# Three of the eight expert blocks at 64 token slots, their high and low halves side by side in one stationary tile

## The chip, the cores and the metric

The kernel runs on one core of one Trainium2 chip. The metric is the device time of one execution in microseconds (us), taken as the median of several runs. The core has TensorE (PE in the profile, its weight loads are PEld), VectorE (DVE), ScalarE (ACT), GpSimd (POOL) and SyncE (SP), which issues nearly all DMAs here.

## The reference, cut to what matters

A decoder of three layers on 256 tokens of width 1024: forgetting attention and a dense SwiGLU; a conformer convolution and a mixture of experts; differential and stick-breaking attention and a squared-ReLU network. All is float32. The change touches the mixture alone.

```python
def moe_swiglu(h, w_router, w_gate, w_up, w_down):     # T = 256, D = 1024, 8 experts, top 2, EXPERT_FF = 3584
    logits = (xt @ w_router).astype(jnp.float32)
    top_logit, top_idx = lax.top_k(logits, TOP_K)
    gates = jax.nn.softmax(top_logit, axis=-1)
    ...
    def expert_block(args):                             # one block of up to 128 tokens of one expert
        xb, e = args
        return (silu(xb @ w_gate[e]) * (xb @ w_up[e])) @ w_down[e]
    ...
    ys = ys * gate_buf[:, None]                         # gate-weighted, added back to the tokens
```

With the reference's own inputs (worked out from its router on the host, no measurement) the eight experts get 87, 54, 67, 80, 49, 43, 66 and 66 of the 512 assignments. None has more than 128, so there are eight blocks. The three smallest of experts 1 to 7 are 5, 4 and 1, with 43, 49 and 54.

## The kernel before

**Exact products.** TensorE multiplies float32 in its fast form only if the operands are rounded. So every operand is split in two: ScalarE writes the rounded, high part (`wh`, `xh`, `ah`), VectorE writes what is left (`wl`, `xl`, `al`; helper `rest`, L2052), and `exact` (L1354 to L1356) adds three products: high by high, high by low, low by high.

**Units.** Weights come as units of 1 MiB (128 partitions by 2048 floats). SP loads each into one of six slots of `raw`; a slot is loaded again when VectorE has split the unit in it (`lo_ready` of six units earlier). ScalarE splits unit j+3 into one of three slots of `wh` when TensorE has finished unit j (`unit_done`), VectorE follows when ScalarE has (`hi_ready`), TensorE when VectorE has (`lo_ready`).

**Blocks.** An expert block is 42 units in the order of `MOE_ORDER`: for each of seven chunks of 512 hidden columns (c = 0 to 6) two halves of gate (g), two of up (u) and, one chunk late, two of down (d). So a chunk is g g u u d d, the down units being those of the chunk before. The tokens' rows, transposed, are the stationary operand (`xgh`, `xgl`, 128 token slots), weights move in 512 columns, and each unit takes 4 pieces x 3 products = 12 matmuls. After g1 ScalarE takes silu of the gate product out of PSUM (L1192); after u1 VectorE multiplies it by the up product (L2539); TensorE turns the 128 by 512 result with four transposes (`turned`, L1839, issued after g1 of the next chunk); ScalarE and VectorE split it (`turned_hi` L1186, `turned_lo`), and the down units use it.

**Loops.** A block number `i` runs over `nb` blocks, read from a register once routing is planned. TensorE and VectorE have one loop over blocks; ScalarE's is turned by a third of a block (`ACT_TURN`), so that it can drain a finished block (L1207) a little into the next. Weight loading is one loop on SP, which takes block i's expert number from `etab`, stores the block's result rows (`y_rows`) at unit 12 of the next and loads the next block's token rows (`x_blk`) at unit 20. `x_rows` and `y_rows` lie in DRAM; their unused rows are zeroed early (`zero_rows`).

**Around the blocks.** Block 0 is expert 0. Its rows are gathered on TensorE by `gather`, a product of the normalised tokens `z_tok` with a selection matrix `sel`. VectorE first plans: `oh` marks each token's experts, `mcum` (TensorE) counts, `kcol` is each assignment's row, `sel` marks the rows of block 0, `kidx` is the list for GpSimd's scatter into `x_rows`, then come `etab`, `nbt` (the numbers of blocks), the gate values, `kept` and `yidx`. Then VectorE splits the gathered rows and the unit `co3`+3, which is unit 2 of block 0, and enters its loop. After the seventh block GpSimd gathers all blocks but the last from `y_rows` (four indirect DMAs), scales by the gates and adds (L784 to L789) while the last block runs; TensorE adds that to the last block's part (`tokens_of_earlier_blocks`, `scatter`).

The set of instructions on each engine is written out by hand in program order; nothing reorders it, and every engine but TensorE's weight loads works it off in that order.

## Time and profile before

| | us |
|---|---|
| median of 3 runs | 1835.2 (1834.9 to 1836.87) |
| span of the profiled execution, first to last instruction | 1835.6 |
| TensorE busy in it | 1801.9 (98%) |
| VectorE busy | 1405.0 (77%) |
| ScalarE busy | 1163.9 (63%) |
| expert loads | 336 of 1 MiB, eight blocks of 42 |

The page gives no other time for the profiled execution, so its span stands for it; it lies 0.4 us over the median. Windows of a trace give busy time, the granted TensorE clock (PEclk, 1.00 is 2.4 GHz and 0.50 is 1.2 GHz) and what the DMA engines moved. "Idle before" is the time that an engine stood before such an instruction, with what ended it.

### The profile page before, as it was taken

Reading aid. Unit: us, or ns where it says so; the run is one execution under the profiler, and the core shown is the slowest. Engines: PE = TensorE matmul, PEld = TensorE weight load, DVE = VectorE, ACT = ScalarE, POOL = GpSimd, SP = SyncE. Lnnn points to the kernel's source line nnn. Section 1 sums busy time; section 2 is a strip of 40 time slices with the busy share of each in tenths; the row PEclk is TensorE's granted clock in tenths of the full one; section 3 lists DMA queues with packets and bytes.
Section 4 is the critical chain, followed back from the end, with each engine's and each line's share of the span. In section 5 each row is a group of like instructions: output and inputs, shape, how many; then the busy total and the mean of one; then the engine's idle time right before and its main releaser. Section 6 shows DMA issues by size and latency. Waiting matters only on the chain.

```text
span 1835.6 us, 28123 instructions
## 1 busy us (share of the span) xinstructions
PE 1801.9 (98%) x10836; PEld 1598.3 (87%) x10836; DVE 1405.0 (77%) x1329; ACT 1163.9 (63%) x1149; POOL 229.4 (12%) x194
## 2 busy tenths in 40 slices
PE   8999999999999999999999999999999999899998
PEld 8988999998878888888888888888887899799997
DVE  6665877679678888888889888888889857665553
ACT  6765434457667777777777777777776757543332
POOL 0462111302020000000000000000007011302221
PEclk9999999999989999999999999999999999999998
DMA  9633888831359999999999999999999943235530
GB/s 391 270 122 145 310 333 328 315 138 39 123 223 385 367 393 381 366 399 373 383 385 374 393 374 370 389 375 392 374 367 420 371 161 138 93 115 184 184 138 24
DMA packets 75407, 523.27 MB, mean 285 GB/s; under 512 B 8296, under 2 KB 8448, under 8 KB 14784
## 3 DMA queue, kind: packets, MB, share of 16 engines
q1 hardware_dynamic: 73056, 514.02, 73.4%
q0 software_dynamic: 2272, 8.15, 1.2%
q8 instruction: 56, 0.92, 0.2%
q14 instruction: 23, 0.19, 0.0%
HBM read 506.38 MB, written 15.75 MB: 284 GB/s over the span
## 4 chain that ended last, share of the span: by engine, by line
PE 93%; DVE 4%; ACT 2%; issue 1%; DMA 0%; POOL 0%; DVEq 0%; SPq 0%; ACTq 0%
PE ps L1354 27%; PE ps L1356 27%; PE ps L1355 27%; DVE wl L2052 1%; PE ps L1677 1%; PE ps L1839 1%; PE ps L1384 1%; ACT wh L828 1%; PE ps L1532 1%; DVE big L2045 1%; PE ps L1368 1%; PE ps L1549 1%; PE ps L1488 0%; PE ps L1377 0%; DMA big<-in_mem 0%
## 5 line engine op out<-in xcount | busy, mean ns | idle before, releaser
L2052 DVE TENSOR_TENSOR wl<-raw,wh 128x2048 fp32r<-128x2048 f32 x446 | 1026.2, 2303 | 261.8 <-ACT wh L828 148.5
L1180 ACT ACTIVATE wh<-raw 128x2048 fp32r<-128x2048 f32 x336 | 644.5, 1919 | 181.8 <-PE ps L1356 181.2
L1354 PE MATMUL ps<-wh,xh 128*128 128x512 f32 (+1 forms) x1040 | 396.3, 381 | 1.7 <-DVE wl L2052 1.7
L1356 PE MATMUL ps<-wh,xl 128*128 128x512 f32 (+1 forms) x1040 | 390.0, 375 | 0.0
L1355 PE MATMUL ps<-wl,xh 128*128 128x512 f32 (+1 forms) x1040 | 389.5, 375 | 0.0
L1354 PE MATMUL ps<-xh,wh 128*128 128x256 f32 x1120 | 321.9, 287 | 5.4 <-DVE xl L2052 3.5
L828 ACT ACTIVATE wh<-raw 128x2048 fp32r<-128x2048 f32 x107 | 204.4, 1910 | 178.2 <-PE ps L1356 174.3
L1355 PE MATMUL ps<-xl,wh 128*128 128x256 f32 x1120 | 317.2, 283 | 0.0
L1356 PE MATMUL ps<-xh,wl 128*128 128x256 f32 x1120 | 317.2, 283 | 0.0
L1354 PEld LDWEIGHTS ps<-wh,xh 128*128 128x128 f32 x1040 | 195.8, 188 | 37.9 <-DVE wl L2052 2.9
L1356 PEld LDWEIGHTS ps<-wh,xl 128*128 128x128 f32 x1040 | 195.7, 188 | 35.6
L1355 PEld LDWEIGHTS ps<-wl,xh 128*128 128x128 f32 x1040 | 195.9, 188 | 33.9 <-issue 0.5
L1354 PEld LDWEIGHTS ps<-xh,wh 128*128 128x128 f32 x1120 | 215.4, 192 | 9.3 <-issue 6.0
L1355 PEld LDWEIGHTS ps<-xl,wh 128*128 128x128 f32 x1120 | 215.3, 192 | 0.6 <-issue 0.5
L1356 PEld LDWEIGHTS ps<-xh,wl 128*128 128x128 f32 x1120 | 215.1, 192 | 0.0
L1354 PE MATMUL ps<-wh,ah 128*128 128x512 f32 x448 | 175.8, 392 | 1.1 <-DVE al L2052 1.1
L1356 PE MATMUL ps<-wh,al 128*128 128x512 f32 x448 | 174.6, 390 | 0.0
L1355 PE MATMUL ps<-wl,ah 128*128 128x512 f32 x448 | 174.4, 389 | 0.0
L1354 PE MATMUL ps<-ah,wh 128*128 128x256 f32 x496 | 142.2, 287 | 0.4 <-POOL al L738 0.2
L1355 PE MATMUL ps<-al,wh 128*128 128x256 f32 x496 | 140.7, 284 | 0.0
L1356 PE MATMUL ps<-ah,wl 128*128 128x256 f32 x496 | 140.6, 283 | 0.0
L738 POOL TENSOR_TENSOR al<-att_p,ah 128x512 fp32r<-128x512 f32 x27 | 74.8, 2771 | 337.9 <-ACT ah L1040 337.9
(327 smaller groups left out, 1978.0 us busy)
## 6 DMA issues: line engine op xcount, KB each, us to landing
raw<-in_experts SPq DMA_DIRECT2D x336, 1024.0 KB, 7.0
raw<-in_units SPq DMA_DIRECT2D x134, 1024.0 KB, 5.3
x_rows<-big SPq DMA_DIRECT2D x1, 6144.0 KB, 36.0
big<-x_rows SPq DMA_DIRECT2D x8, 512.0 KB, 7.8
y_rows<-big SPq DMA_DIRECT2D x7, 512.0 KB, 8.5
y_rows<-big SPq DMA_DIRECT2D x1, 2560.0 KB, 41.7
sqz<-gate_rows POOLq DMA_DIRECT2D x12, 192.0 KB, 4.3
big<-in_mem SPq DMA_DIRECT2D x1, 1024.0 KB, 7.1
```

The lines of the kernel that those rows point to most:

```text
L738: pool.tensor_tensor(al[:, c % 2, :], sg[:, c % 2, :], ah[:, c % 2, :].bitcast(F32), ALU.subtract).then_inc(sem("hid_lo"), 1)
L828: act.activation(wh[:, p % SPL, :], raw[:, n % RAW, :], ACT.Copy).then_inc(sem("hi_ready"), 1)
L1180: act.activation(wh[:, p % SPL, :], raw[:, n % RAW, :], ACT.Copy).then_inc(sem("hi_ready"), 1)
L1354: mm(out_, lh, rh, start=start, stop=False, **kw)
L1355: mm(out_, lh, rl, start=False, stop=False, **kw)
L1356: return mm(out_, ll, rh, start=False, stop=stop, **kw)
L1368: ins = pe.transpose(bank(name)[:, at:at + P], src, ident)
L1384: ins = mm(bank(f"nsum{k}")[:, t:t + 1], src[:, at:at + P], ones[:, 0:1], start=(c == 0 and t == 0), stop=(c == KT - 1), skip_group_check= ...
L1532: ins = mm(s[:, at:at + nk], m["q"][:, P * t:P * t + P], m["k"][:, 0:nk], start=True, stop=True)
L1549: mm(o, m["v"][0], pT[:, 0:T], start=True, stop=False, skip_group_check=True)
L1677: mm(bank(f"conv{c}")[:, 0:T], diag[:, n % DIAG_RING, :], upad[:, c, tap:tap + T], start=(tap == 0), stop=(n + 1 == taps_through(PE_CONV, ...
L2052: return V.tensor_tensor(out_, whole, leading.bitcast(F32), ALU.subtract)
```

## The change

Blocks are numbered anew. Expert 0 stays block 0. The other seven are ranked by their counts on the chip (`order`, `rank`); the three smallest become blocks 1, 3 and 5 with 64 token slots each ("thin"), the next three blocks 2, 4 and 6, the largest block 7. The loops of TensorE, VectorE and ScalarE run three times over a pair (a full block, a thin block), and then over the remaining full blocks.

In a thin block the stationary tile is `thin_x`: columns 0 to 63 are the high halves of 64 tokens, columns 64 to 127 their low halves. Each unit takes two products for each piece, with `wh` and with `wl`, so 8 matmuls and no third product. The partitions of the result are then 64 rows by the high and 64 by the low half, which must be added. For gate and up ScalarE copies both products out of PSUM (`thin_gate`, `thin_up`), and TensorE multiplies each by a constant `fold` (128 by 64, two unit matrices above each other): eight float32 matmuls with 64 moving columns, which add the halves and turn the tile at once. Silu, product and split then work on 256 columns. For the down product the halves are not added on the chip's block: both are stored in `y_rows`, and GpSimd gathers twice, first the low halves of thin blocks into `y_low` (after block 5 is stored; other tokens read a zero row), then as before and adds.

```diff
@@ zero_rows (SP)
-                sp.dma_start(y_rows[E - 1:MAXBLK + 1, :, :]...
+                sp.dma_start(y_rows[2 * THIN:MAXBLK + 1, :, :]...
@@ gpsimd
+            pool.wait_ge(sem("y_stored"), 2 * THIN * 16 + 1)
...
-                                            bass.IndirectOffsetOnAxis(yidx[:, a, t:t + 1], 0)).then_inc(
+                                            bass.IndirectOffsetOnAxis(ylow[:, a, t:t + 1], 0)).then_inc(
...
+                pool.tensor_tensor(y_low[:, t, :], y_got[0][:, t, :], y_got[1][:, t, :],
+                                   ALU.add).then_inc(sem("y_low"), 1)
+            pool.wait_ge(sem("y_low"), TT)
+            pool.wait_ge(sem("y_stored"), last * 16 + 1)
...
+                pool.tensor_tensor(y_low[:, t, :], y_low[:, t, :], y_got[0][:, t, :], ALU.add).then_inc(sem("y_low"), 1)
+                pool.wait_ge(sem("y_low"), TT + t + 1)
+                pool.tensor_tensor(y_kept[:, t, :], y_low[:, t, :], y_got[1][:, t, :],
@@ scalar, thin_units
+                for j in range(first, end):
+                    kind, c, half = MOE_ORDER[j]
+                    if (kind, half) == ("g", 1) and c >= 1:
+                        folded_hi(c - 1)
...
+                    if kind in "gu" and half == 1:
+                        act.wait_ge(sem("unit_done"), past(MOE_UNITS) + POS0 + j + 1)
+                        taken_to, b = (thin_gate, 2 * (c % 2)) if kind == "g" else (thin_up, 2 * (c % 2) + 1)
+                        act.activation(taken_to[:, c % 2, :], ps[:, b, :], ACT.Copy).then_inc(sem("thin_taken"), 1)
+                    split_unit(j, past)
+                    if (kind, half) == ("g", 0) and c >= 1:
+                        folded_silu(c - 1)
@@ tensor, thin_block
+                def both(out_, rows, w, start, stop):
+
+                    mm(out_, rows, w[0], start=start, stop=False)
+                    return mm(out_, rows, w[1], start=False, stop=stop)
+
+                def folded(c):
+
+                    pe.wait_ge(sem("thin_taken"), own(2 * MOE_CH) + 2 * c + 2)
+                    psum, done = spare(f"T{c}", past)
+                    for g, src in enumerate((thin_gate, thin_up)):
+                        for f in range(4):
+                            at = THIN_CAP * (4 * g + f)
+                            ins = mm(psum[:, at:at + THIN_CAP], src[:, c % 2, P * f:P * f + P], fold, start=True, stop=True)
...
+                        if half == 0:
+                            pe.wait_ge(sem("thin_lo"), own(MOE_CH) + c + 1)
...
+                    if (kind, half) == ("g", 0) and c >= 1:
+                        folded(c - 1)
@@ vector, the plan
+            for t in range(TT):
+                V.tensor_scalar(sel[:, t, :], iota, plan_f[:, 1, E * t:E * t + 1], plan_f[:, 0, E * t:E * t + 1],
+                                ALU.is_equal, ALU.mult).then_inc(sem("moe_sel"), 1)
...
+            link(stt(order, cnt, float(E), cc(C_RANK, E), ALU.mult, ALU.add))
+            link(V.tensor_tensor(lt8[:, :, :], inner(order), outer(order), ALU.is_lt))
+            link(V.tensor_reduce(rank, lt8[:, :, :], AX_X, ALU.add))
...
+            gathered_rest(1)
             dve.wait_ge(sem("moe_keys"), 1)
...
+            split_after("co3")
+
+            link(V.tensor_tensor(through, before, over, ALU.add))
@@ vector, thin_block
+                for j, (kind, c, half) in enumerate(MOE_ORDER):
...
+                    split_unit(j, past)
+                    if (kind, half) == ("g", 0) and c >= 1:
+                        folded_product(c - 1)
+                    if (kind, half) == ("g", 1) and c >= 1:
+                        folded_lo(c - 1)
```

**ScalarE, one chunk of a block.** Before, L1180 is the split of a weight unit, L1192 the silu after g1 and L1186 the turned hidden tile's high half.

```order
L1191 REGISTER_ALU
L1192 ACTIVATE att_p<-ps 128x512 [waits unit_done]
L1180 ACTIVATE wh<-raw 128x2048 [waits unit_done,ring_loaded4]
L1185 ISA
L1186 ACTIVATE ah<-ps 128x512 [waits moe_filled7]
L1179 REGISTER_ALU [waits ring_loaded5]
L1180 ACTIVATE wh<-raw 128x2048 [waits unit_done]
```

Now, in a thin block, L1213 is the split of a weight unit, L1253 the silu and L1259 the high half of the folded hidden tile, L1272 a copy of a product out of PSUM; `moe_drained6` is given by VectorE's product.

```order
L1253 ACTIVATE att_p<-ps 128x256 [waits moe_filled6]
L1258 REGISTER_ALU
L1259 ACTIVATE ah<-att_p 128x4x64 [waits moe_drained6]
L1270 REGISTER_ALU
L1272 ACTIVATE att_p<-ps 128x512 [waits unit_done]
L1213 ACTIVATE wh<-raw 128x2048 [waits unit_done,ring_loaded4]
L1212 REGISTER_ALU [waits ring_loaded5]
L1213 ACTIVATE wh<-raw 128x2048 [waits unit_done]
```

The high half and a copy now stand ahead of the split of g1's third-next unit, and the high half waits for VectorE.

**VectorE, the same place.** L2201 is the rest of a weight unit, L2756 the product of silu and up, the row behind L2761 the rest of the folded tile.

```order
L2201 TENSOR_TENSOR wl<-raw,wh 128x2048 [waits hi_ready]
L2756 TENSOR_TENSOR att_p<-att_p,ps 128x256 [waits thin_silu]
L2714 REGISTER_ALU
L2201 TENSOR_TENSOR wl<-raw,wh 128x2048 [waits hi_ready]
L2761 REGISTER_ALU
L2201 TENSOR_TENSOR ah<-att_p,ah 128x4x64 [waits moe_hid_hi]
```

The product stands behind a weight unit's rest, and the next row is a rest that waits for ScalarE.

**VectorE, the plan.** Behind the rest of the second gathered half comes the unit of `co3`+3, and then what is left of the plan, down to `ylow`, before the loop's first weight unit (first rows and last):

```order
L2201 TENSOR_TENSOR xl<-ps,xh 128x512 [waits gather_hi]
L2663 CAST kidx<-kcol 128x4 [waits moe_keys]
L2201 TENSOR_TENSOR wl<-raw,wh 128x2048 [waits hi_ready]
L2666 TENSOR_TENSOR plan_f<-plan_f 128x8
L2667 TENSOR_SCALAR pexp<-plan_f 128x1 [waits dve_step]
...
L2706 TENSOR_SCALAR klow<-klow 128x4 [waits dve_step]
L2707 CAST ylow<-klow 128x4 [waits dve_step]
L2779 UNCONDITIONAL_BRANCH
```

Some thirty small instructions now stand between that unit and the loop, where four stood before; of those ahead of it some twelve are new or moved.

## Rows read from the trace of the kernel before

**Rows 1.** The page: busy time (share of the span) of each engine.

```profile
PE 1801.9 (98%) x10836; PEld 1598.3 (87%) x10836; DVE 1405.0 (77%) x1329; ACT 1163.9 (63%) x1149; POOL 229.4 (12%) x194
```

**Rows 2.** Groups by line, 640 to 1360 us: xcount | busy us, mean ns | idle before.

```profile
L2052 DVE TENSOR_TENSOR wl<-raw,wh 128x2048 fp32r<-128x2048 f32 x256 | 585.8, 2289 | 85.6 <-ACT wh L1180 85.6
L1180 ACT ACTIVATE wh<-raw 128x2048 fp32r<-128x2048 f32 x256 | 491.2, 1919 | 135.4 <-PE ps L1356 135.4
L1354 PE MATMUL ps<-wh,xh 128*128 128x512 f32 x685 | 269.9, 394 | 0.0
L1192 ACT ACTIVATE att_p<-ps 128x512 f32<-128x512 f32 x43 | 25.8, 599 | 34.5 <-PE ps L1356 34.5
```

**Rows 3.** Timeline in a full block: start us, us, engine, line.

```profile
640.57 0.39 PE L1354 MATMUL ps<-wh,xh 128*128 128x512 f32 x1
640.77 1.92 ACT L1180 ACTIVATE wh<-raw 128x2048 fp32r<-128x2048 f32 x1 [0.80 <-PE ps L1356]
641.25 0.39 PE L1354 MATMUL ps<-wh,xh 128*128 128x512 f32 x1
...
642.72 2.29 DVE L2052 TENSOR_TENSOR wl<-raw,wh 128x2048 fp32r<-128x2048 f32 x1 [0.43 <-ACT wh L1180]
...
646.21 0.60 ACT L1192 ACTIVATE att_p<-ps 128x512 f32<-128x512 f32 x1 [0.80 <-PE ps L1356]
...
646.70 1.91 ACT L1180 ACTIVATE wh<-raw 128x2048 fp32r<-128x2048 f32 x1
...
648.64 4.53 DVE L2052 TENSOR_TENSOR wl<-raw,wh 128x2048 fp32r<-128x2048 f32 x2 [0.91 <-ACT wh L1180]
```

**Rows 4.** Timeline of ScalarE: the drains of two blocks that follow each other.

```profile
650.75 1.06 ACT L1207 ACTIVATE big<-ps 128x512 f32<-128x512 f32 x2
769.22 1.06 ACT L1207 ACTIVATE big<-ps 128x512 f32<-128x512 f32 x2
```

**Rows 5.** Small operations elsewhere: timeline, and the last from the chain.

```profile
480.80 0.40 ACT L1135 ACTIVATE xh<-big 128x256 fp32r<-128x256 f32 x1
481.36 0.42 DVE L2052 TENSOR_TENSOR xl<-big,xh 128x256 fp32r<-128x256 f32 x1
503.28 0.98 PE ps L1384 x8
```

**Rows 6.** Stretches: us, busy us of each engine, granted clock, DMA share, GB/s.

```profile
14.00:17.00 3.00, 0.66 (x6) 0.45 (x5) 2.96 (x6) 1.21 (x3) 0.00 (x0) 1.00 0.99 414
17.00:21.00 4.00, 4.00 (x35) 4.00 (x36) 4.00 (x12) 2.62 (x7) 0.00 (x0) 1.00 1.02 421
512.00:515.00 3.00, 0.01 (x1) 0.00 (x0) 2.67 (x16) 2.98 (x5) 0.00 (x0) 0.93 0.00 0
515.00:518.00 3.00, 2.75 (x13) 2.78 (x14) 2.06 (x17) 0.35 (x2) 1.70 (x2) 0.50 0.13 52
```

**Rows 7.** The plan: VectorE's timeline, ScalarE's `z_tok`, and the chain's gather.

```profile
511.43 2.42 ACT L1161 ACTIVATE big<-ps,rcol 128x512 f32<-128x512 f32 x4 [0.62 <-DVE rcol L2083]
515.19 0.17 DVE L2493 TENSOR_TENSOR plan_f<-plan_f 128x8 f32<-128x8 f32 x1
515.25 6.73 PE ps L1786 x32
527.12 2.29 DVE L2052 TENSOR_TENSOR wl<-raw,wh 128x2048 fp32r<-128x2048 f32 x1 [0.89 <-ACT wh L1180]
```

**Rows 8.** A stretch in which the loads lag behind.

```profile
1400.00:1410.00 10.00, 8.92 (x42) 7.04 (x41) 9.08 (x5) 7.40 (x6) 9.92 (x3) 1.00 1.02 424
```

**Rows 9.** Timeline of the last block's end pieces and of GpSimd's pass in it.

```profile
1342.27 0.60 PE L1847 MATMUL ps<-cst,big 128*128 128x128 f32 x4
1403.05 2.58 POOL L789 TENSOR_TENSOR big<-big 128x1024 f32<-128x1024 f32 x1
1411.43 11.43 DVE L2052 TENSOR_TENSOR wl<-raw,wh 128x2048 fp32r<-128x2048 f32 x4
1464.03 0.60 PE L1847 MATMUL ps<-cst,big 128*128 128x128 f32 x4
```

More of the change, by code:

```diff
@@ L71 @@
 MAXBLK = E + EXTRA
+THIN = 3
+THIN_CAP = CAP // 2
+SLOT_OF_RANK = ([2 * r + 1 for r in range(THIN)] + [2 * f + 2 for f in range(THIN)]
+                + list(range(2 * THIN + 1, E)) + [0])
 FF2 = 4096
@@ L96 @@
 C_XI = C_LT + E * E
-C_END = C_XI + EXTRA * E
+C_FOLD = C_XI + EXTRA * E
+C_RANK = C_FOLD + THIN_CAP
+C_SLOT = C_RANK + E
+C_END = C_SLOT + E
 def constants():
@@ L322, in build @@
         y_kept = y_got[0]
+        y_low = view(0, TT, D, sqz)
         sq4 = big[:, 5888:7936]
@@ L1840, in turned @@
                     ins.then_inc(done, 1)
-                def next_rows(g):
-                    psum, done = spare(f"G{g}")
-                    for f in range(4):
-                        at = 512 * g + P * f
-                        ins = pe.transpose(psum[:, P * f:P * f + P], x_blk[:, at:at + P], ident)
-                    ins.then_inc(done, 1)
                 for j, (kind, c, half) in enumerate(MOE_ORDER):
                     if j < 2:
-                        b = MOE_BANK[f"G{half}"][0]
-                        pe.wait_ge(sem(f"moe_drained{b}"), i * len(MOE_USES[b]) + 1)
+                        rows_ready(half, past)
                     if kind in "gu":
                         b = 2 * (c % 2) + (kind == "u")
-                        w = unit(j, 4)
+                        w = moe_unit(j, 4, past)
                         for k in range(4):
@@ new lines, in _ @@
+            with pe.Fori(0, THIN) as i:
+                fat_block(lambda per: i * (2 * per), lambda per: i * per)
+                thin_block(lambda per: i * (2 * per) + per, lambda per: i * per)
+            pe.wait_ge(sem("moe_plan"), 2)
+            nb = pe.value_load(nbt[0:1, 0:1], min_val=E, max_val=MAXBLK)
+            more = pe.value_load(nbt[0:1, 2:3], min_val=E - 2 * THIN, max_val=MAXBLK - 2 * THIN)
+            with pe.Fori(0, more) as i:
+                fat_block(lambda per: i * per + 2 * THIN * per, lambda per: i * per + THIN * per)
@@ L2461, in _ @@
             dve.wait_ge(sem("moe_marks"), 1)
-            pos = plan_f[:, 1, :]
-            cnt = bank("mcum")[:, 2 * E:3 * E]
+            pos, cnt, order, rank = plan_f[:, 1, :], plan_f[:, 4, 0:E], plan_f[:, 2, 0:E], plan_f[:, 3, 0:E]
+            thin, cap, place, over = plan_f[:, 6, 0:E], plan_f[:, 7, 0:E], plan_f[:, 8, 0:E], plan_f[:, 11, 0:E]
+            before, past_cap, through = plan_f[:, 5, 0:E], plan_f[:, 16, 0:E], plan_f[:, 15, 0:E]
             V.tensor_tensor(pos, bank("mcum")[:, 0:2 * E], marks, ALU.subtract)
-            link(stt(lt8[:, :, 0:E], cnt.unsqueeze(1).broadcast_to([P, E, E]), float(CAP),
-                     cc(C_LT, E * E).rearrange("p (a b) -> p a b", a=E), ALU.is_gt, ALU.mult))
@@ L2473, in _ @@
-            link(V.tensor_tensor(two(12), two(10), plan_f[:, 11, 0:E].unsqueeze(1).broadcast_to([P, TT, E]), ALU.add))
+            V.tensor_copy(cnt, bank("mcum")[:, 2 * E:3 * E]).then_inc(drained("mcum"), 1)
+            wait_drained(dve, "mcum")
+            iota = cc(C_IOTA, CAP)
+            for t in range(TT):
+                V.tensor_scalar(sel[:, t, :], iota, plan_f[:, 1, E * t:E * t + 1], plan_f[:, 0, E * t:E * t + 1],
+                                ALU.is_equal, ALU.mult).then_inc(sem("moe_sel"), 1)
@@ new lines, in _, with gathered_rest @@
+            link(V.tensor_tensor(lt8[:, :, :], inner(over), cc(C_LT, E * E).rearrange("p (a b) -> p a b", a=E), ALU.mult))
+            def gathered_rest(j):
+                dve.wait_ge(sem("gather_hi"), j + 1)
+                rest(four_of(xgl, j), bank(f"gather{j}"),
+                     four_of(xgh, j)).then_inc(sem(f"moe_drained{MOE_BANK[f'G{j}'][0]}"), 1)
+            gathered_rest(0)
+            link(V.tensor_reduce(before, lt8[:, :, :], AX_X, ALU.add))
+            link(V.tensor_tensor(past_cap, before, place, ALU.subtract))
```

327 lines of the change are left out of this document (230 added, 97 removed).

## The prediction

> **What bounds the kernel now.** I read the page first: TensorE is busy for 1801.9 of 1835.6 us, VectorE for 1405.0, ScalarE for 1163.9 [rows 1]. Busy alone is no bound, so I looked at who waits in the stretch from 640 to 1360 us, where six blocks run alike. The reader is to see three things there [rows 2]. TensorE's matmuls have no idle time before them. VectorE stood 85.6 us, always for ScalarE, and ScalarE stood 135.4 us, always for TensorE. So TensorE sets the pace and the other two follow it. Its matmuls of 512 columns start 0.227 us apart (three in 0.68 us, [rows 3]), a unit of 12 takes 2.73 us, and a block takes 118.47 us, drain to drain [rows 4], or 16.9 us for a chunk of six units.
>
> Then I asked how far behind the followers are. ScalarE's split takes 1.92 us, VectorE's rest 2.29 us [rows 3]. Where two rests follow each other without a wait they take 4.53 us together, 2.24 each (I use 2.21 for one in a longer run: the second starts 0.08 before the first has ended). Six of them are 13.3 us of the chunk's 16.9. The loads are close too: with loads lagging, the DMA engines move 424 GB/s [rows 8], so 1 MiB needs 2.48 us, and a block with its rows 42 x 2.48 + 2 x 1.28 = 106.7 us.
>
> **The change, part by part.** *TensorE in a thin block.* A unit falls from 12 to 8 matmuls, 8 x 0.227 = 1.82 us. A fold is eight float32 products, each two records. The nearest row for records that small is 0.98 us for 8 [rows 5], so 16 x 0.1225 = 1.96 us; its streaming alone could be half of that. A chunk is 6 x 1.82 + 1.96 = 12.9 us instead of 16.9. If TensorE alone counted, three blocks would save 3 x 7 x 4 = 84 us. It doesn't: the followers now lead.
>
> *The circle in a thin chunk.* I follow VectorE through one chunk, in program order. It does the rest of g0's third-next unit, and behind it the product of 256 columns (0.42 us by [rows 5], 0.35 when next in line). Only then may ScalarE make the high half, since it waits for that product; behind the high half stands the copy of the gate product, and only behind that the split that VectorE needs next. So VectorE stands for 0.31 (high half, 0.40 in [rows 5] less overlap) + 0.49 (copy: 646.21 to 646.70 in [rows 3]) + 1.92 (split) and three hand-overs of some 0.05 (642.69 to 642.72 in [rows 3] is one): 2.9 us. The rest is work: 6 x 2.21 + 2 x 0.35 = 13.96. Together **16.85 us per thin chunk, against 16.9 of a full one**. ScalarE and TensorE fit into the circle: after the standstill VectorE's rests lie back to back, and from a rest (TensorE starts), through a unit (8 matmuls, the last ending 0.39 after its start: 2.0), the split (1.92) to the third-next rest there are 0.3 to 0.4 us to spare in each turn. So by its works alone a thin block lasts 118.3 +- 1.5 us, three of them save 0 (from -5 to +5, if the copy, product or halves are a quarter shorter or longer). The loads need 106.7 and stay hidden.
>
> *The clock.* TensorE has 16.9 - 12.9 = 4.0 us idle in each thin chunk, and most of it in one piece: it has done u1 when VectorE comes out of its standstill, and d0 needs VectorE's rest of that unit and the folded rest behind it. That is 3.1 us; 0.3 before each following unit are the remainder. What do such gaps do? After a stretch with 0.66 of 3.0 us busy (a gap of 2.3 us) the clock stayed at 1.00; after one with 0.01 of 3.0 us busy it was at 0.50 [rows 6], that is 1.2 for 2.4 GHz. Mine lies between them, nearer to the second in length, and it comes 21 times. If the clock falls, the unit behind the gap takes 8 x 0.427 = 3.4 us instead of 1.8 (512 columns at 1.2 GHz are 0.427), 1.6 later; 0.35 is spare, so the circle grows by 1.25 us: 21 x 1.25 = +26 us. I take this, since the gap repeats in the same place and once the clock is down the rest of that chunk is later still; bounds 0 and, with a fall that covers two units each time, 21 x 2.6 = 55 us.
>
> The Trainium skill (TensorE: Matmul & The Clock Gate, Why this matters for your kernels) speaks against the change here: thin matmul bursts parted by waits make the clock oscillate, once with each burst. By that rule the sum is the 1868 below, without it 1841; the trace of before has no such repeated bursts and cannot show it.
>
> *The plan.* `sel` is made some 2 us earlier, but the gather also needs `z_tok`, whose last copy ends at 513.85; it began at 515.25 [rows 7]. So it starts at most 1.2 us earlier. VectorE doesn't follow: after the second gathered half (about 522) come `kidx`, the rest of unit 2 (to 524.5) and some 30 instructions of 0.17 us [rows 7], 5.1 us, so the rest of unit 3 begins at 529.6 instead of 527.12 and ends at 531.9. TensorE had begun unit 3 at 521.98 + 3 x 2.73 = 530.2. **+2 us**, from 0 (small instructions overlap) to 3.5. `kidx` and GpSimd's scatter are 7 us later; the rows are read 17 units later, hidden. Queued behind the plan on VectorE is only its loop.
>
> *GpSimd's second pass.* The last block lasted 1464.03 - 1342.27 = 121.76 us between equal pieces [rows 9], 3.3 more than 118.47, with GpSimd's gather and sums beside it: four rests took 11.43 us there instead of 8.8. Block 6 now gets such a pass too, +3.3, and block 7's has two more additions of 2.58 us; at the same 30% they cost VectorE 1.5, +1.2 after its slack. **+4.5 us**, from 1 (if only the last block feels it) to 8. SP's zeroing is 0.5 MB longer at about 60 us, where loads have idle DMA before them; 0. The waits for `moe_plan` go from ahead of the block loops to behind the first three pairs; VectorE had long given the signal when TensorE ended its gather at 521.98: 0.
>
> The sum against the runs' median (the span is 0.4 more): 1835.2 + 0 + 26 + 2 + 4.5 = **1867.7**, I say 1868.
>
> **The rivals.** *The clock holds.* For it: 3.1 us is shorter than the gap that is known to bring it down, and full work surrounds it. Then 1835.2 + 2 + 4.5 - 0.5 = 1841, 1836 to 1846. Chance 0.20.
>
> *Thin blocks run at VectorE's or the loads' pace (faster).* If the standstill isn't there (ScalarE runs ahead, hand-overs overlap), VectorE needs 42 x 2.21 + 14 x 0.35 + 1.4 = 99 us, loads 106.7, and the block would be 106.7: 3 x 11.8 = 35 saved, 1835.2 - 35 + 6.5 = 1806; half of it gives 1824. For it: VectorE has 13.9 us of work in a chunk. Against: ScalarE's program order. It decides from a standstill under 2.3 us, where a thin chunk beats a full one by enough for the 6.5 us. Chance 0.13.
>
> *The clock stays down longer* (slower still): 1835.2 + 55 + 6.5 = 1897. Chance 0.05. *It doesn't do what it says*: with more than 64 tokens for a thin expert there is a ninth block, +118, 1953. The counts 43, 49 and 54 speak against it. Chance 0.01. The forecast keeps 0.61, from 1853 (half of the gaps bring the clock down) to 1880 (all do, and both other bounds).
>
> **How the numbers follow.** The range takes in the forecast's bounds and the first rival's lower end, 1834 to 1880: 0.61 + 0.19 and little of the second. A measurement of this kernel can tell about 0.2%, 3.7 us, from no change. Faster by more: the second rival, 0.13. Within 1831.5 to 1838.9: the low part of the first, 0.06. Slower: 0.81.
>
> **What would show it.** In the trace after: the distance of two drains with a thin block between them, 118 + 127 us for a pair if I am right, 118 + 118 if the clock holds, 118 + 107 if the second rival is. VectorE's wait before a weight rest, for ScalarE, of 2.9 us once in a thin chunk; ScalarE's wait for VectorE's product before the high half; TensorE's wait for the folded rest of 3.1 us or more seven times a block; granted clock under 1.00 in thin blocks alone. The start of unit 3 near 532, and some 121 us for blocks 6 and 7. The prediction is wrong if VectorE has no such wait, or if the clock stays at 1.00.

## The result, and the profile after

The changed kernel took 1888.05 us (median of four runs, 1887.33 to 1888.5), the kernel before in the same comparison 1835.05 (1833.1 to 1836.87): 1.0288 times the time, 95% interval 1.0275 to 1.0301. It is slower, as forecast, but by 53 us and not by 33, and the time lies above the range. The profiled execution took 1887.85 us, with a span of 1886.0. In all runs whose span is on record it is 1.8 to 1.9 us shorter than the time, so the execution of before whose profile was kept, with its span of 1835.6, took about 1837.4 us and was 2.4 slower than its median. That is why the spans below differ by 50.4 us and the medians by 53.

The page's busy line of after, where [rows 1] stood for before, says that TensorE is busy for 33 us less and that this was no use:

```profile
PE 1769.3 (94%) x10584; PEld 1562.6 (83%) x10584; DVE 1402.5 (74%) x1350; ACT 1167.6 (62%) x1188; POOL 274.2 (15%) x207
```

The groups by line of after from 640 to 1360 us (count | busy us, mean ns | idle before and who ended it) answer to [rows 2]. Before, TensorE's matmuls had no idle time there. Now one group of the thin blocks, the first products of unit d0 with the folded tile, has 64.9 us, and VectorE stands longer for ScalarE:

```profile
L2201 DVE TENSOR_TENSOR wl<-raw,wh 128x2048 fp32r<-128x2048 f32 x243 | 555.7, 2308 | 120.0 <-ACT wh L1213 119.6
L1213 ACT ACTIVATE wh<-raw 128x2048 fp32r<-128x2048 f32 x243 | 460.6, 1914 | 125.4 <-PE ps L1447 67.6 <-PE ps L1984 54.2 <-DMA raw<-in_experts 3.3
L1983 PE MATMUL ps<-wh,ah 128*128 128x512 f32 x168 | 88.6, 527 | 64.9 <-DVE ah L2201 64.9
```

The timeline of after in one thin chunk (start us, us, engine, line, what ended the idle time) shows the circle that the prediction drew:

```profile
686.25 0.41 DVE L2756 TENSOR_TENSOR att_p<-att_p,ps 128x256 f32<-128x256 f32 x1
686.69 0.42 ACT L1259 ACTIVATE ah<-att_p 128x256 fp32r<-128x256 f32 x1 [2.79 <-DVE att_p L2756]
687.02 0.58 ACT L1272 ACTIVATE att_p<-ps 128x512 f32<-128x512 f32 x1
687.49 3.70 ACT L1213 ACTIVATE wh<-raw 128x2048 fp32r<-128x2048 f32 x2
...
689.43 2.29 DVE L2201 TENSOR_TENSOR wl<-raw,wh 128x2048 fp32r<-128x2048 f32 x1 [2.77 <-ACT wh L1213]
...
691.64 0.42 DVE L2201 TENSOR_TENSOR ah<-att_p,ah 128x256 fp32r<-128x256 f32 x1
...
692.21 0.57 PE L1983 MATMUL ps<-wh,ah 128*128 128x512 f32 x1 [3.25 <-DVE ah L2201]
```

VectorE gives the product at 686.66, ScalarE waited 2.79 us for it, and then it makes the high half, the copy and only then the split; VectorE stands 2.77 us; TensorE gets the folded rest after 3.25 us of waiting. The stretches of after around it (us, busy of PE, PEld, DVE, ACT, POOL, granted clock, DMA share, GB/s) show what that gap costs: full clock up to it, half (1.2 GHz) for most of the next 4 us, then full again.

```profile
686.00:689.00 3.00, 2.96 (x14) 2.10 (x12) 0.66 (x2) 2.31 (x3) 0.00 (x0) 1.00 0.99 358
689.00:692.00 3.00, 0.00 (x0) 0.00 (x0) 2.57 (x3) 3.00 (x4) 0.00 (x0) 1.00 0.87 325
692.00:696.00 4.00, 3.79 (x10) 3.00 (x11) 4.00 (x3) 1.68 (x2) 0.00 (x0) 0.57 0.80 296
696.00:703.00 7.00, 7.00 (x41) 6.05 (x40) 5.71 (x4) 5.72 (x4) 0.00 (x0) 1.00 1.02 424
```

The drains of after, beside [rows 4] (a thin block between the first two, a full one between the next):

```profile
659.53 1.06 ACT L1285 ACTIVATE big<-ps 128x512 f32<-128x512 f32 x2
793.20 1.06 ACT L1285 ACTIVATE big<-ps 128x512 f32<-128x512 f32 x2
910.06 1.06 ACT L1285 ACTIVATE big<-ps 128x512 f32<-128x512 f32 x2
```

A pair takes 250.5 us instead of 236.9. How the 250.5 divide between the thin and the full block depends on where a block is said to begin. I mark blocks by the end of VectorE's rest of their first unit, read from the timeline of each kernel:

| us | before | after | products added (e3_fill) | split first (e2_split_first) |
|---|---|---|---|---|
| start of block 0 | 492.55 | 501.02 | 501.23 | 500.21 |
| block 0 | 146.66 | 148.55 | 148.47 | 148.56 |
| blocks 1 to 5 | 592.33 | 628.41 | 596.18 | 566.84 |
| of them the thin ones | (118.47) | 130.39, 127.54, 129.42 | 117.89 each | 107.73, 107.77, 107.80 |
| block 6 | 118.46 | 120.80 | 122.82 | 123.77 |
| block 7 | 121.76 | 125.12 | 124.71 | 125.00 |

So the 50.4 us by which the span grew are 8.5 before the experts, 1.9 in block 0, 36.1 in blocks 1 to 5, 2.3 and 3.4 in the last two blocks, and 1.7 less behind them. The marks leave one thing out. In before the clock was at half from 504 to 508 us, behind the mark of block 0, and in after from 477 to 481, ahead of it; neither kernel has the other's fall:

```profile
504.00:508.00 4.00, 4.00 (x14) 1.48 (x14) 0.00 (x0) 0.28 (x1) 0.00 (x0) 0.57 0.00 0
```

```profile
477.40:480.80 3.40, 3.40 (x8) 2.77 (x9) 1.42 (x4) 0.00 (x0) 0.00 (x0) 0.50 0.51 214
```

The lateness of after against before, matmul by matmul, is therefore 0.7 us from 30 us on, 6.2 behind the stretch of 70 to 90 us, 6.8 from 200 us on, 8.5 at the mark, 6.85 again just ahead of the gather of block 0, and 10.4 in block 0 behind its third unit.

### The profile page after: what moved, and what is told of

It is laid out like the page before. It is cut to its first block, busy times and chain, and to the rows that moved or that the text cites. A ratio compares the mean times of both kernels' runs of the same rounds, so it can differ in the third digit from the quotient of the medians.

```text
span 1886.0 us, 27737 instructions
## 1 busy us (share of the span) xinstructions
PE 1769.3 (94%) x10584; PEld 1562.6 (83%) x10584; DVE 1402.5 (74%) x1350; ACT 1167.6 (62%) x1188; POOL 274.2 (15%) x207
## 4 chain that ended last, share of the span: by engine, by line
PE 75%; DVE 9%; issue 7%; ACT 6%; DMA 2%; POOL 1%; DVEq 0%; ACTq 0%; SPq 0%
PE ps L1445 20%; PE ps L1447 19%; PE ps L1446 19%; DVE wl L2201 5%; ACT wh L1213 4%; PE ps L1983 4%; PE ps L1984 3%; PE ps L1768 1%; PE ps L1475 1%; PE ps L1993 1%; PE ps L1943 1%; DMA raw<-in_experts 1%; ACT wh L867 1%; PE ps L1468 1%; DMA sqz<-gate_rows 1%
## 5 line engine op out<-in xcount | busy, mean ns | idle before, releaser
L2201 DVE TENSOR_TENSOR wl<-raw,wh 128x2048 fp32r<-128x2048 f32 x446 | 1029.9, 2323 | 300.0 <-ACT wh L1213 148.5
L1213 ACT ACTIVATE wh<-raw 128x2048 fp32r<-128x2048 f32 x336 | 638.9, 1915 | 186.0 <-PE ps L1447 128.2
L1445 PE MATMUL ps<-wh,xh 128*128 128x512 f32 (+1 forms) x704 | 265.9, 378 | 15.2 <-DVE wl L2201 10.6
L1447 PE MATMUL ps<-wh,xl 128*128 128x512 f32 (+1 forms) x704 | 259.9, 369 | 0.0
L1446 PE MATMUL ps<-wl,xh 128*128 128x512 f32 (+1 forms) x704 | 259.6, 369 | 0.0
L1445 PEld LDWEIGHTS ps<-wh,xh 128*128 128x128 f32 x704 | 133.2, 189 | 41.6 <-DVE wl L2201 13.7
L1447 PEld LDWEIGHTS ps<-wh,xl 128*128 128x128 f32 x704 | 133.0, 189 | 22.6
L1446 PEld LDWEIGHTS ps<-wl,xh 128*128 128x128 f32 x704 | 133.4, 189 | 21.3 <-issue 0.5
L1983 PE MATMUL ps<-wh,ah 128*128 128x512 f32 x168 | 88.6, 527 | 64.9 <-DVE ah L2201 64.9
L1983 PE MATMUL ps<-wh,xh 128*128 128x512 f32 x336 | 134.6, 401 | 2.3 <-DVE wl L2201 1.8
L1984 PE MATMUL ps<-wl,xh 128*128 128x512 f32 x336 | 131.4, 391 | 0.0
## 6 DMA issues: line engine op xcount, KB each, us to landing
y_rows<-big SPq DMA_DIRECT2D x1, 3072.0 KB, 43.2
```

The source lines that it names most:

```text
L1213: act.activation(wh[:, p % SPL, :], raw[:, n % RAW, :], ACT.Copy).then_inc(sem("hi_ready"), 1)
L1445: mm(out_, lh, rh, start=start, stop=False, **kw)
L1446: mm(out_, lh, rl, start=False, stop=False, **kw)
L1447: return mm(out_, ll, rh, start=False, stop=stop, **kw)
L1983: mm(out_, rows, w[0], start=start, stop=False)
L1984: return mm(out_, rows, w[1], start=False, stop=stop)
```

## Experiments on the thin blocks

**Fill the gap.** If it is the clock that makes a thin chunk 18.4 us (the six long waits of TensorE in the first thin block end 18.4 us apart on average), useless work in the gap must make it shorter.

```diff
+FILL = 3
...
@@ tensor, thin_block
                     else:
+                        if half == 0:
+                            for _ in range(FILL):
+                                mm(ps[:, 2 * (c % 2), :], ident, cc(0, 512), start=True, stop=True)
                         w = moe_unit(j, 2, past)
                         if half == 0:
```

> The changed kernel, with three float32 products of 512 columns on constants added on TensorE in each thin chunk, ahead of its wait for unit d0, into an unused bank; the output is the same. They fill the gap with work that nobody needs. Theory (21 falls of the clock are what makes a thin block 129 us instead of 118, VectorE's circle does the rest): the clock stays at 1.00 in thin blocks, a thin block lasts 118.5, three of them 33 us less, the full blocks behind them 4 less, the time 1852 to 1857. Rival (the clock's fall costs nothing on the path, the handovers do): 1888, or more by the products' own time, 21 x 2.6 = 54.

Measured: 1858.04 us (1855.39 to 1861.0), 1.0122 times before, interval 1.0101 to 1.0143, 1 us over the expected range. The timeline of this kernel has the added products where the gap was (first row: the last three of the six records that the three products leave):

```profile
670.81 1.45 PE L2009 MATMUL ps<-cst 128*128 128x512 f32 x3
...
673.60 0.47 PE L1984 MATMUL ps<-wh,ah 128*128 128x512 f32 x1 [1.34 <-DVE ah L2205]
```

A stretch of thin blocks, of after and then of this kernel:

```profile
670.00:775.00 105.00, 84.59 (x354) 69.47 (x355) 79.69 (x46) 71.24 (x58) 0.00 (x0) 0.84 0.92 355
```

```profile
660.00:750.00 90.00, 85.98 (x381) 63.03 (x382) 75.34 (x44) 69.17 (x56) 0.00 (x0) 1.00 0.98 388
```

The clock is 1.00 instead of 0.84, and each thin block takes 117.89 us, 16.84 a chunk. Adding work that nobody needs made the kernel 30 us faster. VectorE's standstill is still there (2.77 us); what is left is the circle's own length, which the prediction had worked out as 16.85. That the two agree to 0.01 us is in part luck: inside the block the products of d0 lie 16.74 us apart, and the block's ends make the rest. The full blocks behind the thin ones, expected 4 us shorter in all, did not get shorter.

**Take the circle apart.** One call moves on ScalarE:

```diff
@@ scalar, thin_units
                 for j in range(first, end):
                     kind, c, half = MOE_ORDER[j]
+                    split_unit(j, past)
                     if (kind, half) == ("g", 1) and c >= 1:
                         folded_hi(c - 1)
...
-                    split_unit(j, past)
```

> The changed kernel, with one edit in the thin blocks: after g1 ScalarE makes the split of the third-next weight unit first, and only then the high half of the folded tile and the copy of the gate product. Nothing is left out. Theory (VectorE's standstill of 2.8 us in each thin chunk is ScalarE's program order, and it makes the gap of 3.2 to 3.9 us on TensorE behind which the clock falls): the standstill shrinks to under 1 us, the clock stays at 1.00 in thin blocks, a thin block lasts 107 to 111 us instead of 129, and the time is 1826, from 1815 to 1851 (the upper end if the loads lag). Rival (thin units themselves, small matmuls and waits, are what is slow): 1885 to 1888.

Measured: 1829.44 us (1826.24 to 1836.6, eight runs), 0.9967 times before, interval 0.9951 to 0.9983. The timeline of this kernel in a thin chunk: VectorE stands 0.76 us instead of 2.77, and TensorE 1.13 instead of 3.25.

```profile
682.87 2.29 DVE L2201 TENSOR_TENSOR wl<-raw,wh 128x2048 fp32r<-128x2048 f32 x1 [0.76 <-ACT wh L1213]
...
685.65 0.47 PE L1983 MATMUL ps<-wh,ah 128*128 128x512 f32 x1 [1.13 <-DVE ah L2201]
```

Its stretch of a thin block:

```profile
660.00:750.00 90.00, 81.30 (x396) 63.79 (x395) 83.70 (x49) 77.66 (x63) 0.00 (x0) 1.00 1.01 416
```

A thin block takes 107.8 us, clock 1.00, and the DMA engines have no idle share left. That is close to the 106.7 that the second rival of the prediction had for the loads, but the loads do not set the whole pace. A chunk takes 14.87 us from early in the block on, which is VectorE's 13.96 us of work and the some 0.8 for which it still stands; ScalarE's splits waited for a load only 8 times between 640 and 1220 us, 3.8 us in all:

```profile
ACT wh L1213 <- DMA raw<-in_experts: 3.8, 8, 0.6
```

VectorE and the loads are about level here. The waits of TensorE in the experts (us in total, times, longest), of after, with the products and with the split first, put the three side by side. Of the 21 places of after 18 are long, 3.2 to 3.9 us; the seventh of each block is 0.5, 1.4 and 0.2:

```profile
PE ps L1983 <- DVE ah L2201: 64.9, 21, 3.9
```

```profile
PE ps L1984 <- DVE ah L2205: 11.4, 18, 1.3
```

```profile
PE ps L1983 <- DVE ah L2201: 28.2, 21, 2.4
```

**What neither removes.** Leaving a thin block costs something. With the products added, blocks 1 to 5 take 3.9 us more than before though the three thin ones are 0.6 shorter each. The full blocks behind them take 121.4 and 121.1 instead of 118.47, and TensorE stands where one begins; the timelines of after and of e3_fill:

```profile
782.87 0.49 PE L1445 MATMUL ps<-wh,xh 128*128 128x512 f32 x1 [2.41 <-issue]
```

```profile
771.73 0.49 PE L1446 MATMUL ps<-wh,xh 128*128 128x512 f32 x1 [1.73 <-issue]
```

Ahead of it VectorE does the last folded rest and the next block's two row rests between weight rests, and in a full block TensorE has no idle time by which to win the loss back. That this order is the cause is argued, not shown: no kernel tests this part by itself.

## Experiments on the rest

**The early shift.** The prediction had 0 us for the longer zeroing; after is 8.5 us late at the mark of block 0, and 5.5 of them come between 70 and 90 us. The timeline of after shows GpSimd's last gate mask late, TensorE waiting for GpSimd's softmax scaling behind it, and the stretch behind that wait is at half clock:

```profile
74.02 2.80 POOL L717 TENSOR_TENSOR sqz<-sqz,cst 128x128 f32<-128x128 f32 x2 [0.82 <-DMA sqz<-gate_rows]
...
78.69 1.12 PE L1459 MATMUL ps<-cst,att_p 128*128 128x128 f32 x4 [4.26 <-POOL att_p L736]
```

```profile
78.00:81.40 3.40, 2.71 (x13) 2.71 (x14) 1.45 (x4) 0.60 (x1) 2.44 (x3) 0.50 0.65 270
```

The kernel before, in the same place, had all masks made by 71.87 and no wait; its last gate load landed at 70.99, that of after at 73.95:

```profile
68.87 3.00 POOL L698 TENSOR_TENSOR sqz<-sqz,cst 128x128 f32<-128x128 f32 x8 [0.59 <-DMA sqz<-gate_rows]
```

The zeroing itself is over by then. It was issued at 10.9 us in before and at 10.6 in after and took 41.7 and 43.2 us to land (last figure of each row of the pages), so it ended near 53 and 54 us, and GpSimd issues its gate loads from 61 us on:

```profile
y_rows<-big SPq DMA_DIRECT2D x1, 2560.0 KB, 41.7
```

```profile
y_rows<-big SPq DMA_DIRECT2D x1, 3072.0 KB, 43.2
```

What it leaves behind is SP's queue of weight loads, 1.2 to 1.6 us later (the load that landed at 68.61 in before landed at 70.24), and those share the engines with the gate loads. Two kernels ask whether the 0.5 MB are the reason. In the first, block 6's rows are written later (behind the load of ci0), and the zeroing is as short as it was:

```diff
@@ sync
-                sp.dma_start(y_rows[2 * THIN:MAXBLK + 1, :, :].rearrange("a p f -> p a f"),
-                             zeros.broadcast_to([P, MAXBLK + 1 - 2 * THIN, D])).then_inc(sem("rows_zeroed"), 16)
+                sp.dma_start(y_rows[E - 1:MAXBLK + 1, :, :].rearrange("a p f -> p a f"),
+                             zeros.broadcast_to([P, MAXBLK + 2 - E, D])).then_inc(sem("rows_zeroed"), 16)
...
```

> The changed kernel, with the early zeroing of y_rows as short as it was before (from row 7 on); the 0.5 MB of block 6's rows are written later, behind the load ci0. Nothing is left out of the computation. Theory (the longer zeroing shares the DMA engines with GpSimd's gate loads, its masks come late, TensorE waits 4.3 us at 78.7 us and its clock falls): the stretch before the experts is 7 to 8.5 us shorter, the wait of 4.3 us is gone, and the time is 1880. Rival (the early shift of 8.5 us is something else, the order of the plan or the place of buffers): 1888, with the same wait.

Measured: 1883.22 us, four runs from 1878.49 to 1888.24, 1.0254 times before, interval 1.0224 to 1.0285. In its profile the wait is gone and the experts begin at 495.28, 5.7 us earlier. The 2.7 that stay come from elsewhere: 0.5 to 0.7 were there before 70 us, and the rest are falls of the clock at 168 and 472 us; the second, 1.6 us, is made up for by the fall that before has behind the mark. The median is 4.8 us under that of the changed kernel, but the runs overlap: one took 1888. The second kernel is the reverse, the old kernel with the longer zeroing and nothing else:

```diff
@@ sync, of the kernel before
-                sp.dma_start(y_rows[E - 1:MAXBLK + 1, :, :].rearrange("a p f -> p a f"),
-                             zeros.broadcast_to([P, MAXBLK + 2 - E, D])).then_inc(sem("rows_zeroed"), 16)
+                sp.dma_start(y_rows[E - 2:MAXBLK + 1, :, :].rearrange("a p f -> p a f"),
+                             zeros.broadcast_to([P, MAXBLK + 3 - E, D])).then_inc(sem("rows_zeroed"), 16)
```

> The kernel before, with one edit: y_rows is zeroed from row 6 on instead of row 7, 0.5 MB more, at the same early place, as the change has it. Nothing is left out. The short zeroing in the changed kernel took the time down by 5 us only, and its runs differed by 10 us (1878 to 1888), so the early wait seems to come in some executions and not in others. Theory (the longer zeroing delays GpSimd's gate loads past the point at which TensorE's clock falls): the wait of about 4 us at 78 us and a granted clock of 0.50 behind it are there, units from 100 us on are 5 to 8 us later, time 1841 to 1844. Rival (the early shift is the changed order of something else): the wait is not there and the time is 1836 as before, within 2.

Measured: 1841.37 us (1838.32 to 1847.06, twelve runs) beside 1836.58 (1834.69 to 1840.65) for the kernel before: 1.0024, interval 1.0015 to 1.0032, so 3 to 6 us. The profile is that of its slowest run, 1847.06. Its timeline has the same wait, and the stretch behind it half the clock:

```profile
78.71 1.11 PE L1368 MATMUL ps<-cst,att_p 128*128 128x128 f32 x4 [4.28 <-POOL att_p L717]
```

```profile
78.70:84.60 5.90, 5.89 (x28) 5.89 (x29) 1.51 (x4) 1.70 (x5) 3.59 (x4) 0.50 0.29 124
```

So the longer zeroing costs 3 to 6 us in the median, and in this execution the experts began at 503.03, 10.5 us late, 6.9 of them from this wait and the clock behind it. It does not follow that the wait needs the longer zeroing: the kernel with three edits below had a short one and a wait of 2.6 us in its profile. How often each kernel has the wait the profiles, one for each, can't tell.

**GpSimd's first pass.** The kernel without it; the low halves of the thin blocks are missing from its output.

```diff
@@ gpsimd
-            for t in range(TT):
-                for a in range(2):
-                    pool.indirect_dma_start(y_got[a][:, t, :], None, y_by_row,
-                                            bass.IndirectOffsetOnAxis(ylow[:, a, t:t + 1], 0)).then_inc(
-                                                sem(f"y_got{t}"), 16)
...
```

> The changed kernel without GpSimd's first pass: the rows of the low halves of the thin blocks are not gathered, gated and added, so that part of the output is left out. Theory (GpSimd's work beside VectorE's rests makes block 6 2.3 us and block 7 3.4 us longer than their like): block 6 takes 118.5 instead of 120.8, block 7 121.8 instead of 125.1, time 5.7 less, 1882. Rival (the pass is hidden, the longer blocks are the loads of thin blocks catching up): 1888.

Measured: 1883.25 us (1878.2 to 1888.05), 1.0248, interval 1.0226 to 1.027. Block 6 takes 118.58 us and block 7 121.80, 5.5 less together, each as before; the median is 4.8 under that of the changed kernel, with overlapping runs. The cost is on VectorE: the rests of block 6 of after take 2.405 us each in place of 2.29, while GpSimd works (groups by line, 1280 to 1398 us):

```profile
L2201 DVE TENSOR_TENSOR wl<-raw,wh 128x2048 fp32r<-128x2048 f32 x42 | 100.5, 2405 | 11.9 <-ACT wh L1213 11.8
```

**The plan.** The last eleven small instructions of the plan (`late_plan`), not the thirty that the text on record has, are moved. It also puts the new place wrongly: "three pairs" are the three pairs of blocks, so they now stand at the head of block 6.

```diff
@@ vector
-            late_plan()
...
             with dve.Fori(0, THIN) as i:
                 fat_block(lambda per: i * (2 * per), lambda per: i * per, True)
                 thin_block(lambda per: i * (2 * per) + per, lambda per: i * per)
+            late_plan()
             dve.wait_ge(sem("moe_plan"), 2)
```

> The changed kernel, with VectorE's late part of the plan (some thirty small instructions) moved to behind the rests of the first three pairs of block 0. Nothing is left out. Theory (TensorE waits 4.3 us for unit 3's rest, of which 2 are the plan's, and its clock falls behind that): the wait at 539 us is back to some 2 us, and the time is 2 to 4 us less, 1884 to 1886. Rival (scatter and row loads, which are then later too, come on the path): 1888 or more.

Measured: 1888.5 us (1886.65 to 1889.21), 1.0278, interval 1.0263 to 1.0293: no gain. Block 0 did get 4.3 us shorter (144.25), more than the 3.0 that the instructions last there, since the clock no longer falls behind a wait of 4.31 us. But block 6 got 5.2 us longer (125.97) and block 7 1.3 (126.38), and the timeline and stretch of block 6 show the same thing in the new place:

```profile
1277.67 0.15 DVE L2695 TENSOR_TENSOR kfl<-kcol,kept 128x4 f32<-128x4 f32 x1
...
1279.45 0.17 DVE L2707 CAST ylow<-klow 128x4 uint32<-128x4 f32 x1
...
1281.20 6.70 DVE L2201 TENSOR_TENSOR wl<-raw,wh 128x2048 fp32r<-128x2048 f32 x3 [1.58 <-ACT wh L1213]
...
1283.55 0.50 PE L1445 MATMUL ps<-wh,xh 128*128 128x512 f32 x1 [2.22 <-DVE wl L2201]
```

```profile
1284.60:1288.00 3.40, 3.40 (x10) 2.63 (x9) 3.30 (x2) 0.00 (x0) 0.00 (x0) 0.50 0.95 345
```

The instructions last 1.95 us, and behind them VectorE stands another 1.58. The row names ScalarE, but from 1279.46 to 1281.16 VectorE's sequencer reads the two block counts of the loop that begins here (`nbt`, L2782 and L2783). In after it reads them at the same place while a weight rest runs, and VectorE does not stand.

**All together.** The three edits, short early zeroing, split first and late plan, in one kernel:

> The changed kernel, with the short early zeroing, ScalarE's split ahead of the high half in thin blocks, and VectorE's late part of the plan behind the first three pairs of block 0. Nothing is left out. Theory (the three causes are apart and their gains add): 1888 - 8 - 62 - 3 = 1815, from 1805 to 1840, faster than the kernel before (1835). Rival (the loads set the pace once VectorE runs freely, or each cause hides another): 1840 or more.

Measured: 1826.03 us (1824.49 to 1828.03), 0.9940, interval 0.9920 to 0.9959. It beats the kernel before, but not by the sum of 1815: thin blocks 107.7 to 107.9, but the full ones behind them 121.8 and 124.6 (with the clock at half from 984 to 991 us in the second), blocks 6 and 7 124.7 and 126.4, and the early wait (2.6 us) was in its profile although the zeroing was short. With the split first alone blocks 6 and 7 take 123.8 and 125.0, so the plan's new place costs 2.3 there and takes 4.6 off block 0 (144.0 for 148.6). The next kernel takes all of y_rows out of the early stretch:

```diff
@@ sync, of the kernel with the three edits
-                sp.dma_start(y_rows[E - 1:MAXBLK + 1, :, :].rearrange("a p f -> p a f"),
-                             zeros.broadcast_to([P, MAXBLK + 2 - E, D])).then_inc(sem("rows_zeroed"), 16)
...
-                    sp.dma_start(y_rows[2 * THIN:E - 1, :, :].rearrange("a p f -> p a f"),
-                                 cc(0, D).unsqueeze(1).broadcast_to([P, E - 1 - 2 * THIN, D])).then_inc(sem("rows_zeroed"), 16)
+                    sp.dma_start(y_rows[2 * THIN:MAXBLK + 1, :, :].rearrange("a p f -> p a f"),
+                                 cc(0, D).unsqueeze(1).broadcast_to([P, MAXBLK + 1 - 2 * THIN, D])).then_inc(sem("rows_zeroed"), 16)
```

> The kernel with the three edits together (split first in thin blocks, short early zeroing, late plan), and now none of y_rows is zeroed early: all of it is written from zeros held on chip behind the load ci0. Nothing is left out. In the three edits' run the early wait was still there, 2.6 us at 76 us, with the clock at half behind it, though the zeroing was as short as before. Theory (the gate loads share the DMA engines with the zeroing): with 1 MB or more less ahead of them they land 2 us or more earlier, the wait at 76 us is gone, the stretch before the experts ends at 492.5 or earlier in every run, and the time is 1819 to 1821, 5 to 7 under that of the three edits (1826), with less spread. Rival (the early wait has another cause): 1826, the same spread of some 4 us.

The constants that it writes are not zero, against the text on record, so what is added for absent low halves is not zero; what it moves is the same. Measured: 1822.81 us (1822.02 to 1823.38, five runs), 0.9918, interval 0.9905 to 0.9931. The gates landed by 65.7 us, the wait is gone, and the experts begin at 494.74; 1819 to 1821 and 492.5 were expected, and the 2.2 us by which 494.74 is later than before are again falls of the clock elsewhere, the largest at 471 us.

The last one zeroes y_rows by a copy of the zeroed x_rows at that later place, and gives the late plan to GpSimd:

```diff
@@ gpsimd, of the kernel above
+            pool.wait_ge(sem("moe_kept"), 1)
+            link(pool.tensor_tensor(kfl[:, :, :], kcol[:, :, :], kept[:, :, :], ALU.mult))
+            pool.tensor_copy(yidx[:, :, :], kfl[:, :, :]).then_inc(sem("moe_kept"), 1)
...
+            pool.tensor_copy(ylow[:, :, :], klow[:, :, :]).then_inc(sem("moe_kept"), 1)
@@ vector
-            late_plan()
```

> The kernel of the three edits and the late zeroing, with two differences: y_rows is zeroed late by a copy of the zeroed x_rows (the run before it wrote constants there that are not zero, so the rows read for absent low halves were wrong in its output), and VectorE's late part of the plan, which there stood at the head of block 6 and not in block 0, is now made by GpSimd, in some twenty small instructions before its first pass. Nothing is left out. Theory (each small instruction of the plan that VectorE does at the head of a block is late for TensorE, 2 us of its own and as much again where the clock then falls): no wait at 530 us but what was there before, block 6 in 121 to 123 us instead of 125.3, time 1817 to 1820 (1822.8 there). Rival (the 125 us of block 6 are GpSimd's pass and the loads, not the plan): 1822 to 1824.

Measured: 1820.21 us (1816.76 to 1825.76, six runs), 0.9911, interval 0.9896 to 0.9926: the fastest of all, 15.6 us under the kernel before. Between it and the one before it the runs overlap, so the times don't show a gain; in the profiles blocks 6 and 7 are 1.6 us shorter each (123.71 and 124.74). Block 6 was to be 121 to 123: without the plan it is as long as with the split first alone (123.77), so what is left there is not the plan, which is what the rival had. TensorE still waits 2.03 us at 529.1 in block 0, for what is left of the plan on VectorE. The stretch of 62 to 68 us of this kernel shows what room there is when none of `y_rows` is zeroed early; in before its DMA share was 1.00:

```profile
62.00:68.00 6.00, 6.00 (x50) 5.90 (x49) 5.47 (x10) 5.91 (x10) 5.31 (x9) 1.00 0.58 198
```

## Why the prediction was wrong in size

| term | predicted | measured in the profile |
|---|---|---|
| SP's longer zeroing (the wait at 78 us and the clock behind it) | 0 | +5.5 |
| falls of the clock elsewhere ahead of the gather | 0 | +1.4 |
| the plan in block 0 | +2 | +3.5 |
| thin blocks by their works, and the way out of them | 0 | +3.9 |
| the clock in the thin blocks | +26 | +32.2 |
| GpSimd's passes | +4.5 | +5.7 |
| behind the experts | 0 | -1.7 |
| sum (measured: rounded terms; the spans give 50.4) | +32.5 | +50.5 |

Three terms make most of the miss: the clock in the thin blocks was mis-sized by 6.2 us, the zeroing was put at nothing and cost 5.5, and the way out of a thin block, 3.9, was not in the sum.

- **What bounds it**: right. TensorE sets the pace before, and the followers lead in a thin block.
- **The circle**: right. "16.85 us per thin chunk" is 16.84 once the clock holds (e3_fill; the last digit is luck, as said there), the standstill of 2.9 us is 2.77, and ScalarE's program order makes it: one moved call takes 2 us of it away and 21 us off each thin block.
- **The clock**: the mechanism was right, the clock fell in thin blocks and nowhere else between 640 and 1278 us. The size was 6 us short, and of two errors: there are six long gaps in a block, not seven, and each costs 32.2 / 18 = 1.8 us for the 1.25 of the sum. The prediction let one unit of 3.4 instead of 1.8 us be late; in 7 of the 18 places the clock stayed down twice or three times as long (6.8 or 10.2 us, for 3.4 in the others), the case that it had kept for the bound. Its ground for the lower end was weak too: the gap of 2.3 us behind which the clock stayed at 1.00 in before [rows 6] is there in every kernel, and in after the clock fell behind it:

```profile
16.60:20.00 3.40, 3.40 (x16) 3.40 (x17) 3.40 (x11) 1.94 (x5) 0.00 (x0) 0.50 1.02 423
```

  The Trainium skill (TensorE: Matmul & The Clock Gate, Why this matters for your kernels) had the side that came true: bursts parted by waits make the clock oscillate, here once with nearly each thin chunk.
- **The way out of a thin block**: missing from the sum, 3.9 us.
- **"SP's zeroing is 0.5 MB longer at about 60 us, where loads have idle DMA before them; 0"** is the step that was wrong in kind: 5.5 us in the profiles, 4.8 between the medians with the long and the short zeroing. The DMA engines had no idle share there: their busy share was 1.01 from 56 to 62 us and 1.00 from 62 to 68 in before. The zeroing ended near 53 us, the weight loads queued behind it moved back, and GpSimd's gate loads, on another queue, had to share the engines with them. The prediction went by the queue that issues the transfer and did not read the stretch.
- **The plan**: +2 was right for the start of unit 3, but as the sum of two things of which the prediction had one, and what follows that start was missing. The timeline of TensorE of after has the gather and the wait for unit 3:

```profile
521.05 5.44 PE L1877 MATMUL ps<-big 128*128 128x128 f32 x32 [2.19 <-ACT big L1200]
```

```profile
539.00 0.80 PE L1445 MATMUL ps<-wh,xh 128*128 128x512 f32 x1 [4.31 <-DVE wl L2201]
```

  The wait costs 4.3. In return the gather, by the shift of 6.85 us that this place has, starts 1.05 us sooner than before and lasts 5.44 us instead of 6.73 [rows 7], since the clock is down for less of it: 4.3 - 1.05 - 1.3 = 1.95, which puts unit 3 at 539.00 - 6.85 = 532.15, near the 532 of the prediction. Behind the wait the clock fell (granted 0.50 from 538.8 to 542.2), which the prediction did not have, and that is another 1.5: 3.5 in all. The table of marks has 1.9 for block 0 only because the fall at 504 us that before has there, 1.6 us, is not in after; that the marks give the predicted 2 is luck.
- **GpSimd's second pass**: near, 5.7 by the blocks and 5.5 by taking it away, for 4.5.
- **The waits for the plan's counts**: 0 was right; the waits of TensorE from 640 to 1280 us name none of them.

The rivals: the clock didn't hold; the loads' pace (106.7) wasn't reached by this kernel, but one moved call comes within 1.1 us of it (107.8). The sum for the clock staying down longer, 1897, was nearer to the time than the forecast, but only in part for its reason: the clock cost 32 us and not 55.

## What to carry to other kernels

When an engine that set the pace gets less to do, work out the circle of the followers and then look for the single piece of idle time that it leaves on TensorE: here gaps of some 3.5 us cost another 1.8 us each, so it is worth more to break the gap up, by program order on the slowest follower, than to shorten the matmuls. Weigh a bulk transfer that nobody waits for by the share of the DMA engines in that stretch and in the ones behind it, and by the small loads of other queues there, not by its own queue. A few small instructions at the head of a stage were late for TensorE at both heads where they stood, and took the reading of the loop's counts with them at the second; on GpSimd, which was idle, blocks 6 and 7 were 1.6 us shorter each, in one profile. And before a difference of 2 us between two profiles is put down to a change, look where the granted clock fell in each: the same short gap brought it down in some executions and not in others.

## What the runs showed of the hardware

- Gaps of 3.2 to 3.9 us on TensorE, with full work on both sides, brought the granted clock to 0.50 in all 18 places of after; gaps of 1.1 us in each chunk of e2_split_first never did. Between them it isn't settled by length alone. Every kernel has a gap of 2.34 us near 16.6 us; behind it the clock fell in the profiles of six (after, e1, e3, e5, e7, e8) and stayed at 1.00 in five (before, e2, e4, e6, e9). In e2_split_first, of three gaps of 2.42 us, the first, before a product at 754.45, left the clock at 1.00, and behind the two before 984.09 and 1213.56 it fell. The first and the second were followed by these two stretches:

```profile
754.50:757.00 2.50, 2.50 (x11) 2.10 (x12) 2.50 (x2) 0.45 (x1) 0.00 (x0) 1.00 1.01 419
...
985.30:988.50 3.20, 3.20 (x9) 2.46 (x8) 1.44 (x2) 1.61 (x1) 0.00 (x0) 0.50 1.00 415
```

- A small instruction on GpSimd can last as long as the VectorE instruction that it meets. In e9_plan_gpsimd one of 0.20 us fell between two rests; another began 0.12 us after the start of a rest of 2.30 us and took 2.26 (the second row has it and the next one, of 0.22, together). Of the small ones of this plan each took 0.2 or 2.1 to 2.3 us:

```profile
541.40 0.20 POOL L805 TENSOR_TENSOR kfl<-kcol,kept 128x4 f32<-128x4 f32 x1
...
541.81 2.56 POOL L808 TENSOR_TENSOR plan_f<-oh,plan_f 128x16 f32<-128x16 f32 x2
```

```profile
541.69 2.30 DVE L2232 TENSOR_TENSOR wl<-raw,wh 128x2048 fp32r<-128x2048 f32 x1 [0.86 <-ACT wh L1244]
```
